# Projection units during the selection search made by seven products of quarters, with the sums on GpSimd

## The chip, the cores and the metric

The kernel runs on one core of one Trainium2 chip. The metric is the time of one execution on the device, in microseconds (us). The engines of a core are TensorE (PE, matrix products), VectorE (DVE), ScalarE (ACT), GpSimd (POOL) and SyncE (SP, which issues most of the transfers). PEld is TensorE's weight load. Each has its own queue of instructions and they meet by semaphores.

## The reference

One inference step of a one-layer decoder, all in float32: RWKV-7 time mixing beside sparse attention whose keys are selected by an indexer, merged by gates, and a gated feed-forward. What matters here is the projection of the 1104 rows (1040 of the prompt, 64 of the sample) and the selection of 256 keys for each prompt row.

```python
h = rms_norm(x, norm1_g) @ w_in              # 1104 x 1024 by 1024 x 5448
p_r, p_a, g_r, g_a = split_cols(h)           # 1792, 1608, 1024, 1024 columns
pm = p_r + (prev - p_r) * rwkv_mu            # prev is p_r one row earlier
sc = einsum('bqhd,bsd->bqhs', qi, ki) * D_IDX ** -0.5
score = einsum('bqhs,bqh->bqs', relu(sc), wi)
_, idx = lax.top_k(where(visible, score, -inf), 256)
out = attention over the selected keys only  # then time mixing, merge, feed-forward
```

## The kernel before

The change lies in one function, `prompt_and_project`, which in the profiled execution runs from about 224 us to 868 us. It does two things side by side: the indexer, the selection and the attention of the prompt rows; and, as work that TensorE can do in between, the part of the projection that gives p_r and both gates.

**The projection** is cut into 90 units. Unit u makes tile t = u // 3 (128 output columns, 30 tiles, of which the first NT = 14 are p_r and 16 are gates) for the column block j = u % 3 of the transposed input `xT` (3 blocks of 368 rows of the input, in `COLS`). A unit is 8 products of a 128x128 block of weights with a 128x368 block of `xT`, summed in one bank of PSUM (`unit`, L437). Weights come by pairs of tiles, 1 MB each, in two buffers `W` (`load`, L372; pair p waits until all units of pair p - 2 are multiplied). ScalarE takes a unit out of PSUM (`evacuate`, L592 for gates, L594 to L602 for p_r: once scaled by 1 - mu into `PMT`, once by mu, shifted by a row, into `PX`). GpSimd adds the two for a whole tile of p_r (L685, L686), and SyncE sends the tile to DRAM.

**The stage in order.** First the dots: 83 pieces of indexer products (L453 on TensorE, a Relu on ScalarE, L614, and a weighted sum on VectorE, L719 and L721), with units 0 to 3 put among them. Then the search: VectorE finds the 256th largest score of each row by 33 rounds over the bits of a float (`bisect`). A round counts the scores above a trial value: one count over the packed last block (L731), six over the other blocks (L736), then it reads the total of the packed one, which TensorE sums over the partitions with one product (`total`, L458, into `dp_PS`; VectorE's copy is L740), and three instructions on 7 values per partition set the next trial value (L755, L757, L760). TensorE meanwhile makes units 4 to 58, that is 55 units or 440 products ("steps"), and does `total(r)` after each 12 steps (`SPACING`), in an order written by hand; 44 steps remain after the last. Then VectorE turns the scores of the first three blocks into masks (`choose`, L773 to L781, L701), and the heads begin: scores, softmax, transposes and values for 65 heads in 33 teams, with the last 31 units between them (`fill_of`). `scores(0)`, the scores of the first head (L478), is put ahead of unit 4; the first head can go on when VectorE has done `peak_of(0)` (L814, L818), and `scores(1)` (L487) waits for that.

A product in float32 stands in the records as two MATMUL and two LDWEIGHTS entries, so 12 steps are x24 there.

The feed-forward of this kernel already makes some of its products in the way that the change brings here: seven products of quarters in place of eight (`block3`, L2313), with part of the sums on GpSimd.

## Time and profile before

| | |
|---|---|
| median of 3 runs | 2758.52 us (2755.36 to 2760.30) |
| the profiled execution, its own time | 2736.69 us |
| its span, first to last instruction | 2734.9 us |
| mean granted TensorE clock | 0.965 |
| busy: PE, DVE, ACT, POOL | 95%, 64%, 29%, 14% |
| all units (L437), busy | 465.9 us |
| the counts of the search (L736), busy | 176.0 us |

The profile is of one execution, 21.8 us below the median of the others (2758.52 - 2736.69). Its page lists busy time by engine, the granted clock by slice, the chain of work that ended last, and groups of instructions; below it are answers of its trace: stretches with the busy time of each engine, timelines, and groups by line and shape. An engine that is 95% busy over the span can still wait at given places, and it is these places that tell what an edit there is worth. "Idle before" in brackets names what the engine waited for.

### The profile page before, as it was taken

Reading aid. Unit: us, or ns where it says so; the run is one execution under the profiler, and the core shown is the slowest. Engines: PE = TensorE matmul, PEld = TensorE weight load, DVE = VectorE, ACT = ScalarE, POOL = GpSimd, SP = SyncE. Lnnn points to the kernel's source line nnn. Section 1 sums busy time; section 2 is a strip of 40 time slices with the busy share of each in tenths; the row PEclk is TensorE's granted clock in tenths of the full one; section 3 lists DMA queues with packets and bytes.
Section 4 is the critical chain, followed back from the end, with each engine's and each line's share of the span. In section 5 each row is a group of like instructions: output and inputs, shape, how many; then the busy total and the mean of one; then the engine's idle time right before and its main releaser. Section 6 shows DMA issues by size and latency. Waiting matters only on the chain.

```text
span 2734.9 us, 49325 instructions
## 1 busy us (share of the span) xinstructions
PE 2589.1 (95%) x19336; PEld 1788.2 (65%) x19336; DVE 1739.7 (64%) x3313; ACT 788.5 (29%) x1725; POOL 391.4 (14%) x574
## 2 busy tenths in 40 slices
PE   8998999999997997898889999998999999999997
PEld 5553566666654323788756997655656666579997
DVE  3555888874533448666668999988762322357666
ACT  2224322124443653111112553012335321221212
POOL 0000111000000000000001663000335441011111
PEclk9999999999998986999999999999999999999999
DMA  8882112131113450000144664443337563533332
GB/s 297 308 292 86 41 64 88 65 103 37 49 41 106 178 162 27 4 27 12 66 146 160 234 241 167 133 122 129 106 133 242 180 201 117 173 124 123 124 124 72
DMA packets 95961, 348.79 MB, mean 128 GB/s; under 512 B 19561, under 2 KB 43977, under 8 KB 74033
## 3 DMA queue, kind: packets, MB, share of 16 engines
q1 hardware_dynamic: 83696, 294.50, 31.3%
q0 software_dynamic: 12032, 51.14, 5.8%
q8 instruction: 153, 2.51, 0.4%
q14 instruction: 80, 0.65, 0.1%
HBM read 289.57 MB, written 55.23 MB: 126 GB/s over the span
## 4 chain that ended last, share of the span: by engine, by line
PE 47%; DVE 7%; DVEq 3%; issue 1%; DMA 1%; POOL 0%; ACT 0%; POOLq 0%; ACTq 0%; SPq 0%
PE banks L2368 6%; PE banks L2281 5%; PE tl_P L2368 4%; PE banks L2313 4%; PE banks L2299 3%; PE tl_P L2313 3%; PE rc_P L1395 3%; PE banks L2213 3%; PE tl_P L2281 2%; DVE arena L2907 2%; DVEq L2905 2%; PE tl_P L2299 2%; DVE tl_v L2901 1%; PE tl_P L2213 1%; PE banks L1407 1%
## 5 line engine op out<-in xcount | busy, mean ns | idle before, releaser
L437 PE MATMUL dp_PS<-base,dp_W 128*128 128x368 f32 x1440 | 465.9, 476 | 0.0
L437 PEld LDWEIGHTS dp_PS<-base,dp_W 128*128 128x128 f32 x1440 | 265.8, 190 | 157.5 <-issue 8.8
L162 PE MATMUL pa_PG<-pa_W,base 128*128 128x402 f32 (+1 forms) x576 | 198.5, 504 | 7.8 <-DMA pa_W<-in_w_dsa 7.7
L736 DVE TENSOR_SCALAR_CACHE_REDUCE dp_EQ<-dp_SCORE,dp_trial 128x1024 f32<-128x1024 f32 (+1 forms) x186 | 176.0, 946 | 19.9 <-issue 0.9
L162 PEld LDWEIGHTS pa_PG<-pa_W,base 128*128 128x128 f32 (+1 forms) x576 | 106.7, 187 | 94.6 <-issue 14.2
L2281 PE MATMUL banks<-base,tl_WU 128*128 128x368 f32 x496 | 157.9, 475 | 0.8 <-DVE base L2960 0.8
L2299 PE MATMUL banks<-base,tl_WD 128*128 128x368 f32 x484 | 154.3, 474 | 0.0
L2901 DVE MAX8 tl_v<-arena 128x8 f32<-128x4100 f32 x32 | 141.8, 4431 | 3.4 <-issue 1.6
L2904 DVE FIND_INDEX8 tl_i<-tl_v,arena 128x8 uint32<-128x4100 f32 x32 | 141.5, 4423 | 0.0
L2907 DVE MATCH_REPLACE8 arena<-tl_v,arena 128x4100 f32<-128x4100 f32 x32 | 141.3, 4414 | 0.0
L2851 POOL DMA_INDIRECT arena<-in_cache_kv,tl_PHT x128 | 122.6, 958 | 109.9 <-PE tl_P L2447 73.8
L2281 PEld LDWEIGHTS banks<-base,tl_WU 128*128 128x128 f32 x496 | 94.0, 191 | 59.5 <-issue 2.8
L2299 PEld LDWEIGHTS banks<-base,tl_WD 128*128 128x128 f32 x484 | 90.5, 190 | 57.1 <-issue 3.7
L2553 ACT ACTIVATE arena<-base 128x368 f32<-128x368 f32 x44 | 22.1, 509 | 270.6 <-DVEq L2944 150.8
L814 DVE CUSTOM_DVE_ANT_0 dp_P<-dp_PS,dp_SCORE 128x1024 f32<-128x1024 f32 (+7 forms) x64 | 48.5, 758 | 66.7 <-PE dp_PS L487 58.8
L2313 PE MATMUL banks<-arena 128*128 128x184 f32 x504 | 85.6, 319 | 1.4 <-DVE arena L3075 1.4
L2225 PE MATMUL banks<-base,arena 128*128 128x368 f32 x256 | 81.3, 473 | 1.5 <-issue 1.1
L2313 PEld LDWEIGHTS banks<-arena 128*128 128x128 f32 x504 | 80.0, 190 | 1.6 <-issue 1.6
L2213 PE MATMUL banks<-arena 128*128 128x368 f32 x240 | 78.5, 480 | 1.1 <-DMA arena<-in_wb 1.1
L2281 PE MATMUL tl_P<-base,tl_WU 128*128 128x368 f32 x240 | 76.8, 473 | 0.0
L2520 POOL TENSOR_TENSOR base<-tl_T 128x368 f32<-128x368 f32 x36 | 30.6, 850 | 302.4 <-ACTq L2603 301.5
L594 ACT ACTIVATE dp_PMT<-dp_PS,dp_rest 128x368 f32<-128x368 f32 x42 | 23.8, 568 | 164.2 <-PE dp_PS L437 164.2
(525 smaller groups left out, 5077.1 us busy)
## 6 DMA issues: line engine op xcount, KB each, us to landing
tl_WU<-in_wu SPq DMA_DIRECT2D x58, 1024.0 KB, 4.9
pa_WQ<-in_wu SPq DMA_DIRECT2D x22, 1024.0 KB, 8.3
wsum<-pa_WS SPq DMA_DIRECT2D x22, 1024.0 KB, 4.9
tl_WD<-in_wd SPq DMA_DIRECT2D x32, 704.0 KB, 4.4
arena<-wsum SPq DMA_DIRECT2D x21, 1024.0 KB, 7.3
dp_W<-in_w_rw SPq DMA_DIRECT2D x15, 1024.0 KB, 5.5
arena<-in_wb SPq DMA_DIRECT2D x24, 512.0 KB, 3.8
arena<-in_wo SPq DMA_DIRECT2D x24, 512.0 KB, 3.8
```

Source lines behind the costliest of these rows:

```text
L162: last = pe.matmul(PG[0:n, c, 0:NC4], xT[:, k, r:r + n], W[:, c, k, :], start=k == 0, stop=k == KD - 1)
L437: last = pe.matmul(bank(f)[:, 0:w], W[:, t // 2 % 2, k, 128 * (t % 2):128 * (t % 2) + 128], xT[:, k, c:c + w], start=k == 0, stop=k == KD - 1)
L736: dve.tensor_scalar(EQ[0:n, 0:m], scored_of(j), values(n, x), None, op, ALU.add, accum_out=result[0:n, x:x + 1])
L2213: last = pe.matmul(out[:, 0:W], WM[:, i % 2, o:o + 128], YT[:, j, k, :], start=k == 0, stop=k == 3)
L2281: last = pe.matmul(out[:, 0:W], WU[:, i % 2, o:o + 128], XN[:, k, :], start=k == 0, stop=k == KD - 1)
L2299: last = pe.matmul(out[:, 0:W], WD[:, i % 3, 128 * e:128 * e + 128], HT[:, f, :], start=f == 0, stop=f == NF - 1)
L2313: last = pe.matmul(out[:, 0:H], weights[:, k, :], moving(k), start=first and k == 0, stop=k == 3, skip_group_check=True)
L2368: last = pe.matmul(out[:, 0:H], weights[:, k, :], moving(k), start=first and k == 0, stop=k == kk - 1, skip_group_check=True)
L2851: pool.indirect_dma_start(out=KV[:, n % 16, t, :], out_offset=None, in_=I["cache_kv"], in_offset=bass.IndirectOffsetOnAxis(ap=PHT[:, 64 * ...
L2901: dve.max(v8[:, :], SC)
L2904: dve.max_index(i8[:, :], v8[:, :], SC)
L2907: dve.match_replace(SC, v8[:, :], SC, TAKEN)
```

## The change

Units 4, 5 and 54 to 58 stay as they are. The 48 units from 6 to 53 (pairs 1 to 8, `PAIRS`) are made in 24 blocks. A block takes two tiles at once (units 6q + j and 6q + 3 + j) and makes them from quarters: weights of 512x128 and `xT` of 512x184. Seven products of four 128x128 by 128x184 multiplications each (28 in all) stand in for 16 of 128x368. Three of the seven accumulate onto another one in PSUM (`FA`, `FB`, `FD`; the fourth bank is `FE`; these are banks 0 to 3), so ScalarE copies a bank between two products (`keep`), and the second product goes on adding.

The sums that the seven products need are all made by GpSimd:

- `mix_rows(j)`, once per column block: four sums of 128x736 over `xT`, into `XF`. Blocks 0 and 1 at the very start of the stage, block 2 early in the search.
- `weights_a`, `weights_b`, `weights_c`, once per pair of tiles: four sums of 128x512, into `WF`.
- per block: `f16` and `f167` (two sums of 128x184) and `finish` (three sums of 128x184), after which ScalarE may run `evacuate` for the two units, now from `STG` in SBUF.
- `mix_tile(t)`, as before (L685 and L686), two for each pair while the pair after it is made.

The ticks that space the totals count 2 for each product of four multiplications, 1 for each step of a plain unit: 24 blocks x 14 + 56 = 392 in place of 440. `scores(0)` moves behind the last total. The buffers share memory: `RL`, `CUM`, `ones`, `P`, `PTS` and `YB` now lie in one array, `room_for`, over which `WF`, `f1` to `f167`, `STG` and `XF` lie too. So `ones` is filled after the search, and VectorE first waits there for the copies of units up to 53. The number of units among the heads stays 31.

```diff
+        PAIRS = range(1, AHEAD // 6)
+        BLOCKS = [(q, j) for q in PAIRS for j in range(3)]
+        by_seven = lambda u: u // 6 in PAIRS
...
+                def seven(m, tick):
...
+                    def multiply(out, weights, e, moving, first, made):
+                        for k in range(4):
+                            last = pe.matmul(out, weights(e, k), moving(k), start=first and k == 0, stop=k == 3,
+                                             skip_group_check=True)
+                        last.then_inc(made, 1)
+                        tick(2)
...
+                    pe.wait_ge(fa_taken, 2 * m - 2)
+                    multiply(FA, raw, 0, left, True, fa_made)
+                    pe.wait_ge(xf_made, j + 1)
+                    pe.wait_ge(wf_made, 3 * q - 2)
+                    pe.wait_ge(fb_taken, 2 * m - 2)
+                    multiply(FB, mixed_w, 1, mix(1), True, fb_made)
...
+                    multiply(FD, mixed_w, 0, mix(0), True, fd_made)
+                    pe.wait_ge(fa_taken, 2 * m - 1)
+                    multiply(FA, raw, 1, low_left, False, fa_made)
...
+                    multiply(FB, mixed_w, 2, mix(2), False, fb_made)
...
+                    multiply(FE, raw, 3, mix(3), True, fe_made)
+                    pe.wait_ge(wf_made, 3 * q)
+                    pe.wait_ge(fd_taken, 2 * m - 1)
+                    multiply(FD, mixed_w, 3, low_right, False, fd_made)
...
-                scores(0)
-                pe.wait_ge(same_in, 16)
-                steps = [(f, k) for f in range(AMONG, AHEAD) for k in range(KD)]
-                for i, (f, k) in enumerate(steps):
-                    unit(f, k, k + 1)
-                    if i % SPACING == SPACING - 1 and i // SPACING < ROUNDS:
-                        total(i // SPACING)
...
+                def tick(n):
+                    spent[0] += n
+                    if spent[0] >= SPACING * (spent[1] + 1) and spent[1] < ROUNDS:
+                        total(spent[1])
+                        spent[1] += 1
...
+                for m in range(1, NBL + 1):
+                    seven(m, tick)
+                for f in range(6 * PAIRS.stop, AHEAD):
+                    for k in range(KD):
+                        unit(f, k, k + 1)
+                        tick(1)
...
                 scores(0)
...
+                def keep_block(m):
+                    if m > 1:
+                        act.wait_ge(f_mid, m - 1)
...
+                    keep(f1, FA, fa_made, fa_taken, 2 * m - 1)
+                    keep(f6, FB, fb_made, fb_taken, 2 * m - 1)
+                    if m > 1:
+                        both(m - 1)
+                    keep(STG[:, 1, H:2 * H], FD, fd_made, fd_taken, 2 * m - 1)
+                    keep(STG[:, 0, 0:H], FA, fa_made, fa_taken, 2 * m)
+                    keep(f7, FB, fb_made, fb_taken, 2 * m)
...
+                def mix_rows(j):
+                    c = COLS[j][0]
+                    high, low, to = xT[:, 0:4, c:c + 2 * H], xT[:, 4:8, c:c + 2 * H], XF[:, j]
+                    pool.tensor_tensor(to[:, 0], high[:, :, H:], high[:, :, 0:H], ALU.subtract)
+                    pool.tensor_tensor(to[:, 2], low[:, :, H:], high[:, :, H:], ALU.subtract)
+                    pool.drain()
+                    pool.tensor_tensor(to[:, 1], low[:, :, H:], to[:, 0], ALU.subtract)
+                    pool.drain()
+                    pool.tensor_tensor(to[:, 3], low[:, :, 0:H], to[:, 1], ALU.subtract)
...
+                def finish(m):
+                    pool.wait_ge(fd_taken, 2 * m)
+                    pool.wait_ge(fe_taken, m)
+                    pool.tensor_tensor(STG[:, 0, H:2 * H], STG[:, 0, H:2 * H], f16, ALU.add)
+                    pool.tensor_tensor(STG[:, 1, H:2 * H], STG[:, 1, H:2 * H], f167, ALU.add)
+                    pool.tensor_tensor(STG[:, 1, 0:H], STG[:, 1, 0:H], f167, ALU.add)
+                    pool.drain().then_inc(f_done, 1)
...
+                mix_rows(0)
+                mix_rows(1)
                 pool.wait_ge(weighted, dots0[0] + len(pieces(0)) + 1)
...
+                mix_tile(0)
+                pool.wait_ge(weighted, len(all_pieces))
+                weights_a(PAIRS[0])
+                weights_b(PAIRS[0])
+                weights_c(PAIRS[0])
+                mix_tile(1)
+                mix_rows(2)
...
-                dve.memset(ones[:, :], 1.0)
                 pad()
...
                 bisect()
+                dve.wait_ge(copied, 6 * PAIRS.stop)
+                dve.memset(ones[:, :], 1.0)
+                dve.drain()
```

On TensorE, where the search begins: `dp_QZ` is the operand of `scores(0)`, `dp_part` and `dp_same` those of a total, `dp_W` a unit's weights. Before:

```order
L453 MATMUL dp_PS<-KIT,base 128x384 x3
L478 MATMUL dp_PS<-base,dp_QZ 128x512 x4
L478 MATMUL dp_PS<-base,dp_QZ 128x16 x2
L437 MATMUL dp_PS<-base,dp_W 128x368 x12
L458 MATMUL dp_PS<-dp_part,dp_same 128x1
```

and now (`dp_room_for` holds the sums of rows and weights):

```order
L517 MATMUL dp_PS<-KIT,base 128x384 x3
L463 MATMUL dp_PS<-base,dp_W 128x368 x12
L522 MATMUL dp_PS<-dp_part,dp_same 128x1
L463 MATMUL dp_PS<-base,dp_W 128x368 x4
L480 MATMUL dp_PS<-base,dp_W 128x184 x4
L480 MATMUL dp_PS<-dp_room_for 128x184 x8
L480 MATMUL dp_PS<-base,dp_W 128x184 x4
L522 MATMUL dp_PS<-dp_part,dp_same 128x1
```

The first total now stands 12 steps behind the last dot, with no scores between, and from the second on six products of four stand between two totals.

On TensorE, where the search ends. Before:

```order
L437 MATMUL dp_PS<-base,dp_W 128x368 x12
L458 MATMUL dp_PS<-dp_part,dp_same 128x1
L437 MATMUL dp_PS<-base,dp_W 128x368 x44
L487 MATMUL dp_PS<-base,QT 128x512 x4
L500 MATMUL dp_PS<-ident,dp_P 128x128 x8
```

and now:

```order
L463 MATMUL dp_PS<-base,dp_W 128x368 x12
L522 MATMUL dp_PS<-dp_part,dp_same 128x1
L463 MATMUL dp_PS<-base,dp_W 128x368 x8
L522 MATMUL dp_PS<-dp_part,dp_same 128x1
L542 MATMUL dp_PS<-base,dp_QZ 128x512 x4
L542 MATMUL dp_PS<-base,dp_QZ 128x16 x2
L551 MATMUL dp_PS<-base,QT 128x512 x4
L564 MATMUL dp_PS<-ident,dp_room_for 128x128 x8
```

The 44 steps between the last total and the second head's scores are gone; the six products of the first head's scores stand there instead.

On GpSimd, from the start of the stage. Before, with `dp_PMT` and `dp_PX` the two scaled copies of a tile:

```order
L675 MEMSET dp_PX 128x1 x2
L679 DMA dp_PACK<-dp_SCORE 16x130 x8
L685 TENSOR_TENSOR dp_PMT<-dp_PMT,dp_PX 128x1040
L686 TENSOR_TENSOR dp_PMT<-dp_PMT,dp_PX 128x64
```

and now, the first rows, and those of the first block of pair 2, with the two tiles of pair 1:

```order
L789 MEMSET dp_PX 128x1 x2
L795 TENSOR_TENSOR dp_room_for<-base 128x736
L796 TENSOR_TENSOR dp_room_for<-base 128x736
L798 TENSOR_TENSOR dp_room_for<-base,dp_room_for 128x736
L800 TENSOR_TENSOR dp_room_for<-base,dp_room_for 128x736
...
L817 TENSOR_TENSOR dp_room_for<-dp_W,dp_room_for 128x512
L857 TENSOR_TENSOR dp_room_for<-dp_room_for 128x184
L833 TENSOR_TENSOR dp_PMT<-dp_PMT,dp_PX 128x1040
L834 TENSOR_TENSOR dp_PMT<-dp_PMT,dp_PX 128x64
L864 TENSOR_TENSOR dp_room_for<-dp_room_for 128x184
```

The two rows of a tile's sum, which stood alone, now stand between the sums of the quarters, and two groups of four long sums stand ahead of everything.

## Rows read from the trace of the kernel before

**Rows 1.** Busy by stretch: us, each engine (instructions), clock, DMA, GB/s.

```profile
400.00:450.00 50.00, 50.00 (x171) 31.29 (x170) 43.28 (x119) 11.63 (x32) 7.27 (x6) 1.00 0.23 84
```

**Rows 2.** Timeline, one round: start, us, engine, line, operation, [idle before].

```profile
543.90 0.16 DVE L740 COPY dp_count<-dp_PS 128x1 f32<-128x1 f32 x1
544.13 0.17 DVE L755 TENSOR_SCALAR dp_step<-dp_count 128x7 int32<-128x7 f32 x1
...
545.33 0.38 PE L458 MATMUL dp_PS<-dp_part,dp_same 128*128 128x1 f32 x2
...
545.57 7.67 PE L437 MATMUL dp_PS<-base,dp_W 128*128 128x368 f32 x24
...
551.66 0.16 DVE L740 COPY dp_count<-dp_PS 128x1 f32<-128x1 f32 x1
```

**Rows 3.** Timeline, last dots and first search round, VectorE and TensorE.

```profile
303.91 4.05 PE L478 MATMUL dp_PS<-base,dp_QZ 128*128 128x512 f32 x12 [1.04 <-ACT dp_RL L614]
...
305.86 0.92 DVE L844 COPY base<-base 64x128 f32<-64x128 f32 x4
...
307.36 0.29 DVE L731 TENSOR_SCALAR_CACHE_REDUCE dp_EQ<-dp_PACK 128x130 f32<-128x130 f32 x1
...
315.63 0.16 DVE L740 COPY dp_count<-dp_PS 128x1 f32<-128x1 f32 x1 [1.99 <-PE dp_PS L458]
```

**Rows 4.** Timeline, end of the search and start of the heads.

```profile
560.97 27.45 PE L437 MATMUL dp_PS<-base,dp_W 128*128 128x368 f32 x88
...
588.38 1.24 DVE L814 CUSTOM_DVE_ANT_0 dp_P<-dp_PS,dp_P 128x1040 f32<-128x1040 f32 x1 [0.20 <-issue]
...
590.04 1.99 PE L487 MATMUL dp_PS<-base,QT 64*128 64x512 f32 x8 [1.61 <-DVEq L819]
```

**Rows 5.** Timeline of TensorE where seven products are already in use.

```profile
1508.11 1.41 PE L2313 MATMUL tl_P<-base,tl_WU 128*128 128x184 f32 x8
...
1516.83 1.41 PE L2313 MATMUL tl_P<-base,tl_WU 128*128 128x184 f32 x8
```

**Rows 6.** Timeline: a VectorE instruction beside one of GpSimd.

```profile
503.06 2.03 POOL L685 TENSOR_TENSOR dp_PMT<-dp_PMT,dp_PX 128x1040 f32<-128x1040 f32 x1 [12.62 <-ACTq L603]
503.13 1.98 DVE L755 TENSOR_SCALAR dp_step<-dp_count 128x7 int32<-128x7 f32 x1
```

**Rows 7.** Two small VectorE groups, 1495:1675: busy us, mean ns, idle.

```profile
L2908 DVE COPY arena<-tl_v 128x8 f32<-128x8 f32 x13 | 3.7, 284 | 0.0
L2909 DVE CAST arena<-tl_i 128x8 f32<-128x8 uint32 x13 | 3.3, 251 | 0.0
```

**Rows 8.** The first over the whole span, ns min/median/max; GpSimd, 1500:1600.

```profile
L2908 DVE COPY arena<-tl_v x32: 159/162/767, 1429.0 to 1950.3; 128x8 f32<-128x8 f32 x32
...
1500.00:1600.00 100.00, 62.49 (x93) 1.00 0.65 241
```

**Rows 9.** The counts of the search, ns min/median/max.

```profile
L736 DVE TENSOR_SCALAR_CACHE_REDUCE dp_EQ<-dp_SCORE,dp_trial x186: 611/946/1280, 316.9 to 558.7; 128x1024 f32<-128x1024 f32 x31, 128x896 f32<-128x896 f32 x31, 128x768 f32<-128x768 f32 x31, 128x640 f32<-128x640 f32 x31
```

**Rows 10.** Timeline: products weighted on VectorE beside a GpSimd sum.

```profile
286.50 2.46 POOL L685 TENSOR_TENSOR dp_PMT<-dp_PMT,dp_PX 128x1040 f32<-128x1040 f32 x1 [27.34 <-ACTq L603]
...
286.86 5.07 DVE L721 SCALAR_TENSOR_TENSOR dp_SCORE<-dp_RL,WI,dp_SCORE 128x128 f32<-128x128 f32 x7
```

**Rows 11.** Timeline, VectorE as the stage begins.

```profile
230.01 0.93 DVE L831 MEMSET dp_ones<- 128x1040 f32 x1 [7.32 <-DMA dp_later<-in_later]
```

**Rows 12.** Groups of GpSimd by shape: busy us, mean ns, idle before.

```profile
L685 POOL TENSOR_TENSOR dp_PMT<-dp_PMT,dp_PX 128x1040 f32<-128x1040 f32 x14 | 31.0, 2217 | 211.3 <-ACTq L603 211.3
...
L2800 POOL TENSOR_TENSOR arena<-arena 128x184 f32<-128x184 f32 x21 | 12.1, 577 | 4.4 <-ACT arena L2619 3.8 <-issue 0.5
...
L2030 POOL TENSOR_TENSOR arena<-tl_WU 128x512 f32<-128x512 f32 x1 | 1.3, 1265 | 117.2 <-DMA tl_WU<-in_wu 117.2
```

**Rows 13.** TensorE after a long idle: us, busy, clock, DMA, GB/s.

```profile
868.00:876.00 8.00, 0.33 (x4) 0.53 0.82 280
...
882.00:885.50 3.50, 3.50 (x16) 0.50 0.82 253
```

More of the change, by code:

```diff
@@ L603, in evacuate, with keep, both @@
                     act.drain().then_inc(copied, 1)
+                def keep(part, bank, made, taken, count):
+                    act.wait_ge(made, count)
+                    act.activation(part, bank, ACT.Copy).then_inc(taken, 1)
+                def both(m):
+                    q, j = BLOCKS[m - 1]
+                    act.drain()
+                    evacuate(6 * q + j)
+                    evacuate(6 * q + 3 + j)
+                def keep_block(m):
+                    if m > 1:
+                        act.wait_ge(f_mid, m - 1)
+                    else:
+                        act.wait_ge(weighted, len(all_pieces))
+                    keep(f1, FA, fa_made, fa_taken, 2 * m - 1)
[5 more added lines that the diff above has]
+                    keep(f7, FB, fb_made, fb_taken, 2 * m)
+                    keep(STG[:, 1, 0:H], FE, fe_made, fe_taken, m)
+                    keep(STG[:, 0, H:2 * H], FD, fd_made, fd_taken, 2 * m)
                 def rectify(j, p):
@@ L654, in _ @@
                         evacuate(d // EVERY)
-                for f in range(AMONG, AHEAD):
+                for f in range(AMONG, 6):
+                    evacuate(f)
+                for m in range(1, NBL + 1):
+                    keep_block(m)
+                both(NBL)
+                for f in range(6 * PAIRS.stop, AHEAD):
                     evacuate(f)
@@ new lines, in mix_tile @@
+                def mix_tile(t):
+                    px, pm = PX[:, t % 2], PMT[:, t % 2]
+                    seqs = px[:, 1 + TP:].rearrange("p (b q) -> p b q", q=9)
+                    later_rows = pm[:, TP:R].rearrange("p (b q) -> p b q", q=8)
+                    pool.wait_ge(copied, nth_copy(3 * t + 2) + 1)
+                    pool.tensor_tensor(pm[:, 0:TP], pm[:, 0:TP], px[:, 0:TP], ALU.add)
+                    pool.tensor_tensor(later_rows, later_rows, seqs[:, :, 0:8], ALU.add)
+                    pool.drain().then_inc(mixed, 1)
@@ L679, in _ @@
                     pool.dma_start(PACK[16 * x:16 * x + 16, :], SCORE[0:16, PW16 * x:PW16 * x + PW16]).then_inc(packed, 16)
[L680 to L687 removed]
+                mix_tile(0)
[5 more added lines that the diff above has]
+                mix_rows(2)
+                for m in range(1, NBL + 1):
+                    q, j = BLOCKS[m - 1]
+                    if m > 1:
+                        finish(m - 1)
+                        if j == 0:
+                            weights_c(q)
+                    pool.wait_ge(fa_taken, 2 * m - 1)
+                    pool.wait_ge(fb_taken, 2 * m - 1)
+                    pool.tensor_tensor(f16, f1, f6, ALU.add)
+                    if j == 0 and m > 1 and 2 * q - 2 < NT:
+                        mix_tile(2 * q - 2)
+                    if j == 2 and q + 1 in PAIRS:
+                        pool.wait_ge(fd_made, 2 * m - 1)
+                        weights_a(q + 1)
+                    pool.wait_ge(fb_taken, 2 * m)
+                    pool.tensor_tensor(f167, f1, f7, ALU.add)
+                    pool.drain().then_inc(f_mid, 1)
+                    if j == 0 and m > 1 and 2 * q - 1 < NT:
+                        mix_tile(2 * q - 1)
+                    if j == 2 and q + 1 in PAIRS:
+                        weights_b(q + 1)
+                finish(NBL)
                 pool.wait_ge(masked, 1)
@@ L692, in _ @@
                 gather_keys(pool, I, E, KX, kx_in, 0)
-                pool.wait_ge(product, NU)
+                pool.wait_ge(product, NU - 2 * NBL)
                 gather_keys(pool, I, E, KX, kx_in, 1)
```

101 lines of the change are left out of this document (78 added, 23 removed).

## The prediction

> **What bounds the kernel now.** I read the stretches first. In the search (about 307 to 567 us) TensorE is busy for the whole of its time and VectorE for 43.3 of 50 us [rows 1]. That looks like a TensorE bound, so I read one round in the timeline. VectorE reads the total at 543.90 and again at 551.66 without an idle time ahead of it: 7.76 us a round. TensorE's 12 steps between two totals are 7.67 us of records [rows 2]. What TensorE needs when nothing holds it shows in the first round: its steps begin behind a row that ends at 303.91 + 4.05 = 307.96, and VectorE, which waits for it there, has the total at 315.63, 7.67 us later [rows 3]. The difference to 7.76 is small, but VectorE has the longer round. So the chain of the search is VectorE's, and TensorE's steps are cover.
>
> Then the end. After the last total TensorE has 27.45 us of steps left, from 560.97 to 588.42, while VectorE counts, makes three masks and comes to the first head at 588.38. The next products of TensorE start at 590.04 after an idle time of 1.61 us put down to VectorE [rows 4]. So the heads begin when VectorE is ready; a shorter row of steps in front of them starts nothing earlier.
>
> **What is removed from TensorE.** Of 440 ticks 392 stay. Seven products run here already: one block of 28 lasts 1516.83 - 1508.11 = 8.72 us [rows 5], that is 14 ticks of 0.623 us. A plain step is (27.45 - 7.67) / 32 = 0.618 us, from rows of 44 and of 12 steps [rows 2, 4]. So a tick costs the same as before and a round still has 12 of them. The removed 48 ticks (30 us) all fall behind the last total, where VectorE sets the time [rows 4]. Worth: 0. TensorE will wait there for about 560.97 to 588, less the 4.05 us of the first head's scores, instead.
>
> **What moving the first scores gives.** They stand ahead of the first steps and cost 4.05 us; VectorE starts its first count at 307.36 and then waits 1.99 us for the total [rows 3]. With the steps 4 us earlier that wait goes. VectorE is next, so I count -2.0 us and not 4.
>
> **What GpSimd adds.** Each edit there costs nothing by itself; the question is who waits for it and whom it stops. For the second there are rows. At 503.13 a VectorE instruction on 7 values took 1.98 us in place of 0.17; a GpSimd sum ran from 503.06 to 505.09, and VectorE's ended 0.02 us behind it [rows 6]. In the dots, seven weighted sums of 128x128 took 5.07 us beside such a sum [rows 10]. Later, where GpSimd is busy for 62 of 100 us, two small VectorE instructions take 284 and 251 ns on average against a median of 162, in the worst case 767 [rows 7, 8]. The counts, which fill most of a round, show no such thing: the longest of 186 takes 1280 ns [rows 9]. So some VectorE instructions wait for a running GpSimd sum to its end: the three small ones of a round, the sums of two arrays, the small copies.
>
> The Trainium skill, page "SBUF — State Buffer", section "Who interferes with whom", says that copies, tensor_scalar without its accumulator and instructions with two SBUF inputs share a port pair with GpSimd, that whoever starts first keeps it for the whole instruction, and that the other blocks fully. It speaks against this change, and rows 6 agree. Taken at its word for each instruction it gives the upper price of the rounds below, 29 us, where rows 7 give 9 to 13.
>
> Now the places, with the durations of [rows 12]: a sum of 128x184 0.577 us, of 128x512 1.27, of 128x1040 2.22; so one of 128x736, which no row has, about 1.65 (between the last two, by length).
>
> 1. Start. `mix_rows(0)` and `mix_rows(1)` are eight sums of 1.65 us, 13 us and some gaps from about 224 on, to about 237. VectorE waits for a transfer until 230.01 [rows 11], so the first half is free. In the other 7 us it has seven small copies and sums to make and then the weighted sums, and gets about one in for each sum of GpSimd. The dots that follow are a chain of VectorE. Between 0 (GpSimd loses each time) and 7 (VectorE stands still); I take 5, nearer to the upper end, because seven short ones beside a single sum of 2.46 us are stretched to 5.07 [rows 10], and here the sums follow one another.
> 2. Start of the search. `weights_a` to `weights_c` are four sums of 1.27 us as soon as the last dot is weighted, when VectorE has seven short instructions to do, such as four copies in 0.92 us [rows 3]. Between 0 and 5; I take 3.5. Then `mix_rows(2)`, four sums of 1.65 us, meets the three small ones of one round: 0 to 5, I take 3.
> 3. The rounds. Blocks last 24 x 14 / 12 = 28 rounds. In three blocks (42 ticks, 3.5 rounds of 7.76 = 27.2 us) GpSimd has fifteen sums of 0.577, four of 1.27 and, for six pairs of eight, two of 2.22. An instruction that comes at any moment waits on average the sum of the squares of these over twice the time: (5.0 + 6.5 + 9.9) / 54.4 = 0.39 us with the long ones, 0.21 without. Three in a round, six pairs of eight: 3 x (0.75 x 0.39 + 0.25 x 0.21) = 1.04 us, times 28 = 29 us. The same sum for the stretch of [rows 7, 8], with some 5 sums of 0.577 and three of 0.9 in each 8.73 us, gives 0.24 us where the rows show (122 + 89) / 2 = 105 ns. By that ratio, 0.44, the rounds cost 13 us; by the 105 ns as they stand, 3 x 0.105 x 28 = 9 us. I take 15: near the rows, and a little over them, as the three come 0.24 us apart and can each meet the next sum of a row of sums. Range 9 to 29.
> 4. `ones`: 0.93 us less at the start [rows 11], 0.93 and a drain more behind the search. +0.1. Its wait for the copies of unit 53 costs nothing: block 24 ends at tick 352, in round 30 of 33.
>
> **The clock.** TensorE's wait of some 23 us (27.4 - 4.05) ahead of the heads is new. After such a gap in this trace the granted clock was 0.50 (1.2 GHz) while TensorE was nearly idle, and stayed there for 3.5 us of full work behind it [rows 13]. That costs half of 3.5 us, or up to 4 if it lasts twice that. Part lies beside the softmax of the first head. +2, range 0 to 4.
>
> **ScalarE** is busy 11.6 of 50 us in the search [rows 1]. Seven copies of 128x184 in a block, even at GpSimd's 0.577 us each [rows 12], bring it to some 6 of 9 us; hidden, unless it waits (rival C).
>
> **The sum.** -2.0 + 5 + 3.5 + 3 + 15 + 0.1 + 2 = +26.6 us. The profiled execution, 2736.7 us, would be 2763.3. The median of the runs before is 2758.52, 21.8 us above that execution; the difference belongs to no place that the trace shows, so I add the sum to the median: 2785.1 us. Ends: -2 + 0 + 0 + 0 + 9 + 0.1 + 0 = +7.1, that is 2765.6, and -2 + 7 + 5 + 5 + 29 + 0.1 + 4 = +48.1, that is 2806.6.
>
> **The rivals.**
> A. The waits behind GpSimd cost next to nothing, because its sums fall beside the counts, as they do now: of fourteen long sums [rows 12] two show someone waiting [rows 6, 10]. For it: the medians of [rows 8] are the undisturbed ones. Against: GpSimd's share goes from 7 of 50 us [rows 1] to two thirds. Then -2 to +5: 2757 to 2764, the same.
> B. It gets faster: TensorE is the bound of the search after all, by its full busy time [rows 1], and 48 ticks of 0.62 us come off. Then 2758.5 - 30 = 2728.5. It decides if the last total came late by TensorE; rows 2 and 4 speak against it, for VectorE waits for nothing there, and the ticks come off behind the last total.
> C. TensorE starves. In a block, the copy of product 3 must be made before product 7, and ScalarE gets to it only behind `both`, which waits for `finish` on GpSimd. If GpSimd and VectorE hold each other up so that a block comes 1 us later than the 9.05 us that VectorE's rounds leave it, 24 blocks add 24 us to the sum: 2809. For it: the long sums of `mix_tile` stand ahead of `finish` in that queue. Against: GpSimd's own work is 18 of 27 us by the prices above, and the same scheme ran at 8.72 us a block in [rows 5].
>
> **How the numbers follow.** Forecast (slower by 7 to 48 us) 0.73, C 0.12, A 0.10, B 0.05. A measurement of this kernel can tell 0.2% (5.5 us) from no change. Faster comes from B, same from A, slower from the forecast and C. The range leaves out B, most of A, and the far end of C: 2762 to 2812.
>
> **What the profile after would show.** The 33 counting rounds longer than 7.76 us on average, about 8.3, with L755, L757 and L760 (or the lines that they have then) at maxima of 0.5 to 2 us and each such end on the end of a GpSimd sum; the counts unchanged. The first weighted sum later than 232.96 by some 5 us. TensorE idle for some 20 us ahead of the heads, with a lower clock behind it. Blocks of 8.7 us with waits only at totals. If VectorE waits for totals in many rounds, C is right; if the small ones keep 0.17 us, A; if the heads start before 588 us by more than 3, B. I am wrong most easily in the 15 us of the rounds, since the phase between blocks and rounds is not random: rounds stand at seven fixed places of three blocks.

## The result, and the profile after

| | before | after |
|---|---|---|
| median | 2759.04 us (2755.36 to 2760.30) | 2777.45 us (2774.77 to 2779.04) |
| ratio | 1 | 1.0074, 95% interval 1.0059 to 1.009 |
| the profiled execution, its own time | 2736.69 us | 2778.36 us |
| its span | 2734.9 us | 2776.6 us |

The change made the kernel slower by 18.4 us (16.3 to 24.8 by the interval), where 26.6 were forecast. The two profiled executions lie 41.7 us apart. The second half of that comes from a place far behind the change, and the last part of this section takes it out.

**Where it comes from.** I put the same instruction side by side in both traces (us from the start of the span; starts).

| anchor | before | after | later by |
|---|---|---|---|
| first weighted sum | 232.96 | 235.61 | 2.6 |
| last weighted sum | 304.6 | 308.4 | 3.8 |
| first count (L731, after L914) | 307.36 | 315.20 | 7.8 |
| first total read (L740, after L923) | 315.63 | 321.56 | 5.9 |
| last total read, 32 rounds on | 567.3 | 585.3 | 18.0 |
| first mask | 567.8 | 587.0 | 19.2 |
| first head on VectorE (L814, after L997) | 588.38 | 607.62 | 19.2 |
| second head's scores (L487, after L551) | 590.04 | 609.27 | 19.2 |
| last product of the stage | 868.1 | 888.5 | 20.5 |

Stage start, the timeline of after (start, us, engine, line, operation, idle before). Before, the four copies took 0.54 us, the two 0.39 and the first weighted sum 0.49:

```profile
229.78 2.08 DVE L976 COPY dp_QZ<-QT 64x32 f32<-64x32 f32 x4
229.80 1.75 POOL L800 TENSOR_TENSOR dp_room_for<-base,dp_room_for 128x736 f32<-128x736 f32 x1
...
232.18 3.02 DVE L983 COPY dp_QIZ<-base 64x64 f32<-64x64 f32 x2
...
235.61 1.76 DVE L902 TENSOR_SCALAR dp_SCORE<-dp_room_for,WI 128x512 f32<-128x512 f32 x1
```

VectorE's small instructions are held one at a time: one of the four copies took 1.71 us and ended 0.03 us behind the sum at 229.80, and the two 64x64 copies (1.33 and 1.68 us) ended 0.05 us behind the sums after it. Start of the search, VectorE and GpSimd, after; it answers to [rows 3], where L844, now L1026, took 0.92 us:

```profile
311.76 1.89 DVE L1026 COPY base<-base 64x128 f32<-64x128 f32 x4
313.66 1.17 DVE L1028 COPY base<-KIT 128x64 f32<-128x64 f32 x1
...
321.56 0.16 DVE L923 COPY dp_count<-dp_PS 128x1 f32<-128x1 f32 x1
```
```profile
312.00 1.34 POOL L813 TENSOR_TENSOR dp_room_for<-dp_W 128x512 f32<-128x512 f32 x1 [0.18 <-issue]
313.51 1.27 POOL L817 TENSOR_TENSOR dp_room_for<-dp_W,dp_room_for 128x512 f32<-128x512 f32 x1 [0.18 <-issue]
```

The first total is read without an idle time ahead of it; the 1.99 us of [rows 3] are gone. Two rounds of the search, after:

```profile
428.59 0.16 DVE L923 COPY dp_count<-dp_PS 128x1 f32<-128x1 f32 x1
428.83 1.05 DVE L938 TENSOR_SCALAR dp_step<-dp_count 128x7 int32<-128x7 f32 x1
...
430.20 1.09 DVE L943 TENSOR_SCALAR dp_trial<-dp_bits 128x7 int32<-128x7 int32 x1
...
438.52 0.16 DVE L923 COPY dp_count<-dp_PS 128x1 f32<-128x1 f32 x1 [0.43 <-issue]
438.76 0.44 DVE L938 TENSOR_SCALAR dp_step<-dp_count 128x7 int32<-128x7 f32 x1
...
439.51 2.23 DVE L943 TENSOR_SCALAR dp_trial<-dp_bits 128x7 int32<-128x7 int32 x1
```
```profile
428.58 1.27 POOL L807 TENSOR_TENSOR dp_room_for<-dp_W 128x512 f32<-128x512 f32 x1 [0.25 <-PE dp_PS L480]
430.00 1.27 POOL L809 TENSOR_TENSOR dp_room_for<-dp_room_for,dp_W 128x512 f32<-128x512 f32 x1
...
438.59 0.58 POOL L857 TENSOR_TENSOR dp_room_for<-dp_room_for 128x184 f32<-128x184 f32 x1 [0.24 <-issue]
439.33 2.38 POOL L833 TENSOR_TENSOR dp_PMT<-dp_PMT,dp_PX 128x1040 f32<-128x1040 f32 x1 [0.17 <-ACTq L687]
```

L938 ends at 429.88 and L807 at 429.85; L943 at 431.29 and L809 at 431.27; L943 at 441.74 and L833 at 441.71. Over the whole search the three small lines and the counts, ns min/median/max:

```profile
L938 DVE TENSOR_SCALAR dp_step<-dp_count x31: 170/172/1051, 329.4 to 578.0; 128x7 int32<-128x7 f32 x31
```
```profile
L943 DVE TENSOR_SCALAR dp_trial<-dp_bits x30: 170/172/2226, 330.1 to 570.7; 128x7 int32<-128x7 int32 x30
```
```profile
L919 DVE TENSOR_SCALAR_CACHE_REDUCE dp_EQ<-dp_SCORE,dp_trial x186: 612/946/1280, 322.9 to 577.1; 128x1024 f32<-128x1024 f32 x31, 128x896 f32<-128x896 f32 x31, 128x768 f32<-128x768 f32 x31, 128x640 f32<-128x640 f32 x31
```

The medians are as before, the maxima are not, and the counts are those of [rows 9]. All 33 small instructions of 0.2 us or more in the search end 0.02 to 0.03 us behind the end of a GpSimd instruction. I also added up, for the stretch from the first to the last read of a total, what the small instructions (128x7) took over 0.172 us each, VectorE's idle time put down to TensorE, and the idle time of its own issue:

| kernel | search, us | small ones over 0.172 us (how many took 0.2 us or more) | wait for TensorE | issue | rest |
|---|---|---|---|---|---|
| before | 251.66 | 1.83 (1 of 94) | 0.20 | 2.26 | 247.37 |
| after | 263.71 | 14.29 (33 of 94) | 0.00 | 1.72 | 247.70 |

So a third of the small instructions carry the 12.05 us (263.71 less 251.66); the rest is only 0.33 us apart. GpSimd is busy for 32.3 of 50 us here, against 7.3 in [rows 1]:

```profile
400.00:450.00 50.00, 45.18 (x276) 43.93 (x275) 43.51 (x104) 21.23 (x65) 32.31 (x39) 0.97 0.23 80
```

The end of the search, after, in the timeline, and the stretches behind the second head's scores (us, PE, PEld, DVE, ACT, POOL, clock, DMA share, GB/s):

```profile
586.00 0.93 DVE L1032 MEMSET dp_room_for<- 128x1040 f32 x1 [0.32 <-issue]
...
607.62 1.24 DVE L997 CUSTOM_DVE_ANT_0 dp_room_for<-dp_PS,dp_room_for 128x1040 f32<-128x1040 f32 x1 [0.20 <-issue]
...
609.27 3.78 PE L551 MATMUL dp_PS<-base,QT 64*128 64x512 f32 x8 [24.37 <-DVEq L1002]
```
```profile
609.00:613.00 4.00, 3.73 (x9) 1.29 (x9) 1.02 (x3) 1.25 (x2) 0.00 (x0) 0.50 0.02 4
613.00:617.00 4.00, 3.73 (x19) 2.57 (x18) 2.77 (x6) 1.46 (x3) 0.00 (x0) 0.97 0.00 0
```

TensorE's idle time in front of L551 is 24.37 us where it was 1.61 [rows 4]: most of the 30 us taken off TensorE is here, as a hole. Behind it the clock is 0.50 (1.2 GHz) for 4 us; the same scores took 1.99 us in [rows 4] and take 3.78 now.

**The other 21 us.** From L2313's last product to L2281's last, far behind the stage, the trace of before has 471.5 us and that of after 492.8. A 50 us window there, of after, then of before:

```profile
2071.00:2121.00 50.00, 30.52 (x115) 18.75 (x116) 6.07 (x20) 12.59 (x26) 22.03 (x24) 0.76 0.55 173
```
```profile
2050.00:2100.00 50.00, 46.77 (x245) 29.60 (x245) 13.04 (x45) 23.44 (x49) 30.68 (x32) 0.97 0.77 245
```

In the window of after TensorE is idle for 19.5 us. The rows put 13.9 us of that down to its own issue, such as this one; one wait for a transfer (3.2 us) and one for ScalarE (2.9 us) stand there too:

```profile
2090.37 0.47 PE L2466 MATMUL banks<-base,tl_WU 128*128 128x368 f32 x1 [2.24 <-issue]
```

All nine experiments below have the long form too (493.5 to 494.5 us), the two made from the kernel before among them. So it is not the change; the profiled execution of before, 22 us faster than the median, was one without it. Like for like the change costs 20.5 us by the traces (the last anchor, which lies ahead of that place) and 18.4 by the medians.

### The profile page after: what moved, and what is told of

Its sections match the earlier page's. It is cut to its first block, busy times and chain, and to the rows that moved or that the text cites. A ratio compares the mean times of both kernels' runs of the same rounds, so it can differ in the third digit from the quotient of the medians.

```text
span 2776.6 us, 51076 instructions
## 1 busy us (share of the span) xinstructions
PE 2575.7 (93%) x19912; PEld 1855.8 (67%) x19912; DVE 1762.9 (63%) x3313; ACT 843.2 (30%) x1893; POOL 520.1 (19%) x738
## 4 chain that ended last, share of the span: by engine, by line
PE 48%; DVE 6%; DVEq 2%; issue 1%; another core or an unknown queue 1%; DMA 1%; ACT 0%; POOL 0%; ACTq 0%; POOLq 0%; SPq 0%
PE banks L2553 6%; PE banks L2466 5%; PE tl_P L2553 4%; PE banks L2498 4%; PE banks L2484 3%; PE tl_P L2498 3%; PE rc_P L1580 2%; PE banks L2398 2%; PE tl_P L2466 2%; PE banks L2410 2%; DVE arena L3092 2%; DVEq L3090 2%; PE tl_P L2484 2%; DVE tl_v L3086 1%; PE banks L1592 1%
## 5 line engine op out<-in xcount | busy, mean ns | idle before, releaser
L463 PE MATMUL dp_PS<-base,dp_W 128*128 128x368 f32 x672 | 222.2, 477 | 1.0 <-ACT dp_room_for L723 1.0
L919 DVE TENSOR_SCALAR_CACHE_REDUCE dp_EQ<-dp_SCORE,dp_trial 128x1024 f32<-128x1024 f32 (+1 forms) x186 | 176.0, 946 | 19.5 <-issue 0.5
L463 PEld LDWEIGHTS dp_PS<-base,dp_W 128*128 128x128 f32 x672 | 122.1, 190 | 74.3 <-issue 8.8
L480 PE MATMUL dp_PS<-dp_room_for 128*128 128x184 f32 x576 | 100.5, 324 | 0.0
L480 PEld LDWEIGHTS dp_PS<-dp_room_for 128*128 128x128 f32 x576 | 92.1, 192 | 0.0
L997 DVE CUSTOM_DVE_ANT_0 dp_room_for<-dp_PS,dp_SCORE 128x1024 f32<-128x1024 f32 (+7 forms) x64 | 48.5, 758 | 68.2 <-PE dp_PS L551 60.8
L691 ACT ACTIVATE dp_room_for<-dp_PS 128x184 f32<-128x184 f32 x168 | 51.0, 325 | 113.0 <-PE dp_PS L480 107.1
```

What stands on the lines that cost most here:

```text
L463: last = pe.matmul(bank(f)[:, 0:w], W[:, t // 2 % 2, k, 128 * (t % 2):128 * (t % 2) + 128], xT[:, k, c:c + w], start=k == 0, stop=k == KD - 1)
L480: last = pe.matmul(out, weights(e, k), moving(k), start=first and k == 0, stop=k == 3, skip_group_check=True)
L919: dve.tensor_scalar(EQ[0:n, 0:m], scored_of(j), values(n, x), None, op, ALU.add, accum_out=result[0:n, x:x + 1])
```

## The experiments

Ratios are to runs of the kernel before made beside each kernel on the same chip, with medians of 2755.1 us (e1, e2, e3, e7), 2755.4 (e4, e5, e8) and 2753.6 (e11, e12); for the change itself it was 2759.04. So compare kernels by their ratios, not by their medians. The search is the stretch between the first and the last read of a total, and the other columns are from one trace each.

| kernel | median, us | ratio, 95% interval | first total read | search | second head's scores | last product of the stage |
|---|---|---|---|---|---|---|
| after | 2777.45 | 1.0074 (1.0059 to 1.009) | 321.6 | 263.7 | 609.3 | 888.5 |
| e1_no_sums | 2758.0 | 1.0014 (1.0001 to 1.0027) | 312.7 | 256.8 | 593.5 | 873.4 |
| e2_psum_bits | 2761.26 | 1.0026 (1.0014 to 1.0038) | 322.0 | 250.8 | 596.8 | 875.6 |
| e3_later_sums | 2772.92 | 1.007 (1.0052 to 1.0088) | 313.5 | 268.5 | 606.0 | 885.1 |
| e4_six_ahead | 2760.22 | 1.0018 (1.0003 to 1.0033) | 321.9 | 264.9 | 610.8 | 872.9 |
| e7_before_short | 2759.82 | 1.0013 (1.0003 to 1.0023) | 315.5 | 251.4 | 589.7 | 868.9 |
| e8_psum_later | 2762.87 | 1.0033 (1.0017 to 1.0049) | 313.0 | 259.7 | 596.6 | 876.8 |
| e5_all | 2750.6 | 0.9983 (0.9971 to 0.9995) | 313.1 | 260.5 | 601.2 | 863.3 |
| e11_bits_six | 2746.0 | 0.997 (0.996 to 0.998) | 321.5 | 250.3 | 597.6 | 856.8 |
| e12_before_six | 2765.56 | 1.0043 (1.0031 to 1.0055) | 315.0 | 251.4 | 617.8 | 877.3 |

**e1_no_sums: are GpSimd's sums the cause?**

```diff
 def mix_rows(j):
-    pool.tensor_tensor(to[:, 0], high[:, :, H:], high[:, :, 0:H], ALU.subtract)
...
+    if j == 0:
+        pool.memset(XF[:, 0].rearrange("p i k n -> p (i k n)"), 0.0)
...
-    pool.tensor_tensor(f16, f1, f6, ALU.add)
...
-    pool.tensor_tensor(f167, f1, f7, ALU.add)
```

> The changed kernel with every sum that GpSimd makes for the seven products left out (mix_rows, weights_a to weights_c, f16, f167, finish; one fill of XF stands in for the first). All waits, products and copies stay, so the units are wrong. Theory (VectorE waits behind GpSimd's sums): rounds of the search back at 7.76 us, the first head (608 us after, 588 us before) at about 587 us, the whole within 0.1% of before. Rival (the chain of products and copies is late, or the cover of TensorE is missed): rounds stay over 8 us and the first head beyond 600 us.

The second head's scores come 15.8 us earlier than in after, the ratio falls from 1.0074 to 1.0014. So the sums are most of it. The first head stands at 591.8, not at the 587 expected. What is left is 3.54 us of small instructions behind the long sums of `mix_tile` (the kernel before had 1.83), and a wait that was covered in after, 4.65 us on VectorE: it reads the total with TensorE late. TensorE, in the timeline of this kernel:

```profile
356.64 0.28 PE L522 MATMUL dp_PS<-dp_part,dp_same 128*128 128x1 f32 x2
358.08 1.49 PE L480 MATMUL dp_PS<-base,dp_room_for 128*128 128x184 f32 x8 [1.16 <-ACT dp_room_for L691]
```
```profile
356.22 0.31 ACT L670 ACTIVATE dp_PX<-dp_sh,dp_mu 128x8 f32<-128x8 f32 x1 [2.60 <-DMA PM_dram<-dp_PMT]
...
357.61 0.98 ACT L691 ACTIVATE dp_room_for<-dp_PS 128x184 f32<-128x184 f32 x4
```

Product 7 stands still because ScalarE copies product 3 only behind `evacuate`. That is rival C's place, but not its reason: GpSimd makes no `finish` sums here. ScalarE had waited 2.60 us for the transfer of an earlier tile to DRAM, whose buffer the new tile needs. The pair of rows comes five times, once in each of five pairs (TensorE waits 1.16 to 2.44 us, ScalarE for the transfer 2.60 to 3.99). This is read from the rows; no run took the transfer away.

**e7_before_short: would fewer steps behind the last total pay by themselves (rival B)?** In the kernel before, units 54 to 58 are one product in place of eight; the rest of these units is left out.

```diff
+if 54 <= f < AHEAD:
+    if end == KD:
+        pe.matmul(bank(f)[:, 0:w], W[:, t // 2 % 2, 0, 128 * (t % 2):128 * (t % 2) + 128],
+                  xT[:, 0, c:c + w], start=True, stop=True).then_inc(product, 1)
+    return
```

> The kernel before with units 54 to 58 cut to one product each in place of eight: 35 of the 44 steps behind the last total are left out, nothing else. Theory (VectorE sets the start of the heads): the first head stays at 588 us; the heads lose at most 1 to 2 us by a lower clock after TensorE's wait; time within 0.1%. Rival (TensorE is the bound there): the heads begin 21 us earlier and the whole is 0.8% faster.

TensorE stops at 567.0 in place of 588.4. The first head does not move:

```profile
588.00 1.24 DVE L819 CUSTOM_DVE_ANT_0 dp_P<-dp_PS,dp_P 128x1040 f32<-128x1040 f32 x1 [0.20 <-issue]
```
```profile
589.66 3.60 PE L492 MATMUL dp_PS<-base,QT 64*128 64x512 f32 x8 [22.68 <-DVEq L824]
```

The scores take 3.60 us in place of 1.99, at a granted clock of 0.51 over 4 us, and the heads last 279.3 us (589.66 to 868.95) in place of 278.0. Rival B is out, and the price of TensorE's wait with the low clock behind it is 1.3 us, apart from the rest of the change. That is one pair of executions; in the other kernels here with such a gap (after, e1_no_sums, e2_psum_bits, e3_later_sums, e8_psum_later) the heads last 278.9 to 280.2 us.

**e2_psum_bits: is it the access to SBUF that the small ones wait for?** The step and the next bit go to bank 7 of PSUM; the third instruction becomes an exclusive or of two arrays, one of them there, and one memset of 7 values is added to a round. The work of GpSimd stays as it is.

```diff
+step_p, next_p = (PS[:, 7, c:c + NS].bitcast(I32) for c in (0, 16))
+dve.memset(next_p, 1 << max(b - 1, 0))
-dve.tensor_scalar(step[:, :], count[:, :], float(TOPK), float(1 << b), ALU.is_ge, ALU.mult)
+dve.tensor_scalar(step_p, count[:, :], float(TOPK), float(1 << b), ALU.is_ge, ALU.mult)
-dve.tensor_tensor(bits[:, :], bits[:, :], step[:, :], ALU.bitwise_xor)
+dve.tensor_tensor(bits[:, :], bits[:, :], step_p, ALU.bitwise_xor)
-dve.tensor_scalar(trial[:, :], bits[:, :], 1 << (b - 1), None, ALU.bitwise_xor)
+dve.tensor_tensor(trial[:, :], bits[:, :], next_p, ALU.bitwise_xor)
```

> The changed kernel with the three small instructions of a round taken off the shared reads and writes: the step and the next bit lie in PSUM, so each has one operand in SBUF only (one tiny fill more in a round). GpSimd's work is the same. Theory: they no longer wait for GpSimd's sums, rounds of 7.8 to 7.9 us in place of 8.24 on average, the first head about 11 us earlier (597 us), the whole 0.4% faster than the changed kernel. Rival (the rounds are long for another reason, such as late totals): rounds stay at 8.2 us.

The search takes 250.78 us, less than before the change: 0.10 us over in 1 of 94 small instructions, where after has 14.29 in 33. Two of the lines, ns min/median/max:

```profile
L940 DVE TENSOR_SCALAR dp_PS<-dp_count x31: 168/168/169, 329.9 to 565.5; 128x7 int32<-128x7 f32 x31
```
```profile
L945 DVE TENSOR_TENSOR dp_trial<-dp_bits,dp_PS x30: 161/162/163, 330.4 to 557.9; 128x7 int32<-128x7 int32 x30
```

They now run inside a sum of GpSimd, in the timeline of this kernel:

```profile
439.72 0.57 POOL L864 TENSOR_TENSOR dp_room_for<-dp_room_for 128x184 f32<-128x184 f32 x1 [0.18 <-issue]
439.73 0.16 DVE L942 TENSOR_TENSOR dp_bits<-dp_bits,dp_PS 128x7 int32<-128x7 int32 x1
439.97 0.16 DVE L945 TENSOR_TENSOR dp_trial<-dp_bits,dp_PS 128x7 int32<-128x7 int32 x1
```

The wait belongs to instructions with all their arrays in SBUF. One array of it in PSUM frees them, and 12.9 us of the 20.5 are back. Of the rest, 6.4 us lie ahead of the first total (322.0 against 315.6).

**e3_later_sums: the dots and the first weights.** `mix_rows(1)` and the first `weights_a` to `weights_c` wait until VectorE has made its small copies.

```diff
 mix_rows(0)
-mix_rows(1)
...
-pool.wait_ge(weighted, len(all_pieces))
+pool.wait_ge(indexed, 1)
 weights_a(PAIRS[0])
 weights_b(PAIRS[0])
 weights_c(PAIRS[0])
+mix_rows(1)
 mix_tile(1)
 mix_rows(2)
```

> The changed kernel with mix_rows(1) taken out of the dots and the first weights_a to weights_c held until VectorE has done its small copies ahead of the search; both now run under the first rounds. Theory: the dots end 4 to 5 us earlier (as before the change), the search begins 4 us earlier, a part comes back as waits in the first rounds (1 to 3 us): the first head at about 601 us. Rival: the rows for block 2 come too late and TensorE, then VectorE, waits: no gain.

The first total is read 8.1 us earlier, at 313.5, and the last only 3.3 us earlier; the first head comes at 604.3, where 601 was expected. The long sums meet the first rounds instead: these last 9.49 and 10.15 us, with small instructions such as

```profile
314.50 1.63 DVE L934 TENSOR_SCALAR dp_trial<-dp_bits 128x7 int32<-128x7 int32 x1
```
```profile
324.40 1.62 DVE L940 TENSOR_TENSOR dp_bits<-dp_bits,dp_step 128x7 int32<-128x7 int32 x1
```

In all 17.55 us over in place of 14.29, and 2.22 us of waits for TensorE. The ratio, 1.007, cannot be told from that of the change. A collision that is moved is mostly paid elsewhere.

**e8_psum_later: both edits.**

> Both repairs without moving units: step and next bit in PSUM, and the first sums held until the search. Theory: dots as before the change (end at 304.5 us), search of 251 to 255 us (the small ones do not wait; TensorE's wait at product 7 for ScalarE may cost 1 to 3 us in the first rounds), the first head at about 588 to 590 us, as before the change; the whole 2757 to 2760 us. So the change without its collisions is worth nothing by itself. Rival: the whole is faster than before by more than 0.2%.

The two gains do not add up: the search lasts 259.7 us, not 251 to 255, and the time is that of e2_psum_bits alone (1.0033 against 1.0026, with intervals that overlap). The small ones are free (1.98 us over, in two instructions), but VectorE waits 7.74 us for TensorE, and TensorE waits for the chain ScalarE, GpSimd, in this kernel's timeline:

```profile
331.05 2.82 PE L480 MATMUL dp_PS<-base,dp_W 128*128 128x184 f32 x8 [4.71 <-ACT dp_room_for L691]
...
365.86 1.49 PE L480 MATMUL dp_PS<-base,dp_room_for 128*128 128x184 f32 x8 [1.83 <-ACT dp_room_for L691]
```
```profile
329.49 0.57 POOL L857 TENSOR_TENSOR dp_room_for<-dp_room_for 128x184 f32<-128x184 f32 x1 [0.24 <-issue]
330.02 0.57 POOL L864 TENSOR_TENSOR dp_room_for<-dp_room_for 128x184 f32<-128x184 f32 x1
```

The first block's `f16` and `f167` (L857, L864) stand behind thirteen long sums of GpSimd and end at 330.59. ScalarE may not overwrite `f1` until then, and the product at 331.05, the fourth of block 2, adds onto the bank that ScalarE has to copy into it. The later rows, at product 7, are those of e1_no_sums. Once VectorE is not the late one, both show.

**e4_six_ahead: is TensorE's freed time worth anything?** Six teams of heads go without a unit, and these six units are made ahead of the heads, 65 in all.

```diff
-return int(m >= 256 or x < NTEAM - 2)
+return int((m >= 256 or x < NTEAM - 2) and x not in (2, 7, 12, 17, 22, 27))
```

> The changed kernel with six units taken out of the heads (teams 2, 7, 12, 17, 22, 27 hold none) and made ahead: 65 units ahead in place of 59, three of the blocks more and one pair more by seven products, 434 ticks. TensorE's wait of 24 us ahead of the heads is filled. Theory (the 48 ticks saved are worth what the heads give up): the heads lose 6 x 5.1 us of products and end about 28 us earlier against their start, the first head comes 1 to 3 us later by three more blocks of GpSimd's sums: the whole about 27 us below the changed kernel, 2750 us, 0.3% below before. Rival (the heads are not bound by TensorE, the units among them fill waits): less than 10 us gained.

It gives 0.56% back (ratio 1.0018 in place of 1.0074, some 15.4 us), not the 28 expected. The heads last 262.1 us in place of 279.3. Their 48 products less are 29.7 us of TensorE at 0.618, and TensorE is busy 27 us less there; 10 us come back as idle time. The rows name the softmax, such as:

```profile
773.63 0.66 PE L564 MATMUL dp_PS<-ident,dp_room_for 128*128 128x128 f32 x4 [1.14 <-DVEq L1011]
777.85 1.09 PE L580 MATMUL dp_PS<-dp_room_for,V 128*64 128x128 f32 x16 [1.58 <-ACTq L746]
```

**e5_all: e8_psum_later with six units more ahead, as in e4_six_ahead.**

> Both repairs and six units fewer among the heads. Theory: the first head at 588 to 592 us, the heads 28 us shorter, the whole about 2731 us, 1.0% below before. Rival: TensorE, now without room in the search, delays the totals (a block waits at product 7), and half of it or more is lost.

The first of these kernels that is faster than before, by 0.17%, but 20 us behind its expectation. The search keeps the 8.57 us of waits for TensorE, the heads give 17 and not 28, and the first head comes 24.2 us behind the first mask in place of 20.6: its scores stand behind the 38 steps that are left after the last total (x76 in the row) and end at 599.54.

```profile
572.01 23.74 PE L463 MATMUL dp_PS<-base,dp_W 128*128 128x368 f32 x76
595.59 3.95 PE L542 MATMUL dp_PS<-base,dp_QZ 128*128 128x512 f32 x12
```

**e11_bits_six: each lesson applied.** GpSimd's sums stay where the change put them, the bits are in PSUM, six units more are ahead, and the first scores stand right behind the last total.

```diff
 for f in range(6 * PAIRS.stop, AHEAD):
     for k in range(KD):
         unit(f, k, k + 1)
         tick(1)
+        if spent[1] == ROUNDS and not asked:
+            pe.wait_ge(fa_taken, 2 * NBL)
...
+            scores(0)
+            asked = True
-for r in range(spent[1], ROUNDS):
-    total(r)
...
-scores(0)
```

> The change with two edits more: the next bit and the step of a round lie in PSUM, and six units more (65 in all) are made ahead of the heads, with the first head's scores right behind the last total and not behind the last unit. Theory (VectorE's small instructions wait for GpSimd in the rounds, and TensorE's freed time is worth something only if heads' units move into it): the search as with the bits in PSUM alone, 250 to 252 us, so the first head at 595 to 597, not held up by its scores; the heads 262 us in place of 279; so 17 us below the run with the bits in PSUM alone: about 2744, ratio to before 0.996. If the early scores hold up the totals or the units behind them, the second head's scores come behind 599 and the gain is 12 us or less: 2749. If the heads gain nothing because their softmax sets the time: 2761.

As expected within 2 us: 2746.0 us, 0.997 of before (0.996 to 0.998). The search takes 250.3 us with no wait for TensorE. TensorE's row behind the last total now reaches 1.7 us too far: the second head's scores start 3.4 us behind the first head (594.19), against 1.65 in the kernels where TensorE is free by then:

```profile
569.37 4.03 PE L542 MATMUL dp_PS<-base,dp_QZ 128*128 128x512 f32 x12
573.25 23.74 PE L463 MATMUL dp_PS<-base,dp_W 128*128 128x368 f32 x76
597.58 1.99 PE L551 MATMUL dp_PS<-base,QT 64*128 64x512 f32 x8 [0.59 <-ACTq L688]
```

The clock stays up too: the scores take 1.99 us. This version is faster than both kernels, by 0.3% against the kernel before.

**e12_before_six: was the seven-product form needed for that?** The kernel before with the same six units moved.

> The kernel before with six units more made ahead of the heads (65 in all), all by eight products. Theory (before, TensorE's row behind the last total, 27.45 us, just covers VectorE's masks; 48 steps more are bare): the second head's scores 28 to 30 us later, near 619, the heads 17 us shorter; slower than before by 11 to 13 us: about 2767, ratio 1.0044. Rival (the units among the heads are the cost and it was the seven products that made no difference): as fast as the change with this edit, 2755 or less.

Slower than before by 0.43%. The row behind the last total is now bare:

```profile
560.08 57.13 PE L437 MATMUL dp_PS<-base,dp_W 128*128 128x368 f32 x184
617.80 1.99 PE L487 MATMUL dp_PS<-base,QT 64*128 64x512 f32 x8 [0.59 <-ACTq L603]
```

The scores stand 27.8 us later, and 18.6 us come back in the heads. So the heads last the same in both kernels (259 us), and the change's 48 ticks are what makes room for the six units. This pair shows what the change is worth when VectorE does not pay for it: 2765.6 against 2746.0 us. The bits in PSUM, which e12_before_six lacks, can explain at most the 1.8 us that its search loses to held instructions. Against the kernel before as it was, the gain is 7.6 us.

## Why the prediction was right, and where its sizes were off

**The bound** (VectorE's chain, TensorE's steps as cover) held. For the row behind the last total e7_before_short and e12_before_six show it from both sides: 21 us less of TensorE gives nothing, 30 us more cost 28. In the search of after VectorE never waits for TensorE, and TensorE waits 8.4 us for VectorE's counts. "Worth: 0" for the 48 ticks was right, and so was the idle time in front of the heads ("some 23 us", 24.37 measured).

**The mechanism** (small VectorE instructions held for the length of a GpSimd sum, counts not) held, with the ends of the rows and with the PSUM version. The Trainium skill's page "SBUF — State Buffer", section "Who interferes with whom", names the port pair that the two engines share; these runs agree on who waits (tensor_scalar, tensor_tensor and copies of SBUF arrays, up to 2.23 us), and on counts with an accumulator not waiting (946 ns in the median, as before). Each term:

| term | forecast | measured |
|---|---|---|
| first total's wait gone | -2.0 | -1.9 (7.8 less 5.9) |
| (1) `mix_rows` in the dots | +5 | +4.7 (3.8, and the 0.93 of `ones` that left) |
| (2) first weights | +3.5 | +4.0 (7.8 less 3.8) |
| (2) `mix_rows(2)` and (3) the rounds | +18 | +12.1 (search), +12.5 in the small ones alone |
| (4) `ones`, at both ends | +0.1 | +0.3 (1.2 less 0.93) |
| the clock | +2 | +1.2 to 1.3 |
| sum | +26.6 | +20.5 in the trace, +18.4 in the medians |

The terms are read from one trace of each kernel, and VectorE's transfer at the start of the stage landed 0.6 us earlier in after, so single terms can be off by that much.

The terms that were too large are `mix_rows(2)` and the rounds. Two parts can be named. First, the kernel before already had 1.83 us of such collisions in the search, nearly all of it in [rows 6]; my sum priced the long sums of `mix_tile` again as if they were new. Second, `mix_rows(2)` was priced at 3 us for one round, and its last sum, up to 329.73, met instructions at 329.41 and 330.07 whose excess is 0.17 and 0.33 us, the second with sums of the block. What is left is 14.0 us for 28 rounds, 0.17 us for each small instruction (12.2 us and 0.15 us without what was there before). It lies between the 0.105 of [rows 7, 8] and the 0.35 that the formula's 29 us come to, and nearer to the rows, as chosen. The 15 us were a choice between two values, not worked out, so that they came within 1 us is in part luck. Whether the phase between blocks and rounds matters, which I named as the weak point, the trace leaves open: the rounds that begin at 353.96, 412.84 and 473.45, seven apart, last 7.99, 7.99 and 8.01 us, but those at 370.05, 428.59 and 489.22, seven apart too, last 8.85, 9.93 and 8.04.

**Rival C** had a right mechanism with no price here. Product 7 does wait for ScalarE, up to 1.79 us at a time in the trace of after (three times), but VectorE's longer rounds cover it: the wait for TensorE in its search is 0.00. It becomes real as soon as VectorE is quick: 4.65 us in e1_no_sums, 7.74 in e8_psum_later. Half of its reason was wrong: where `finish` was named, the rows at product 7 name the transfer of a tile. **Rival A** fell (33 of 94 instructions took 0.2 us or more), **rival B** too (e7_before_short).

**The median.** I wrote that the 21.8 us between the profiled execution and the median belonged to no place that the trace shows. One trace could not show it; beside the later ones it has a place, TensorE's idle time near 2090 us. Adding the sum to the median was right; comparing the two spans would have doubled the answer.

What stays open: what causes that idle place and makes it come and go between executions, and whether heads with fewer units could be ordered to lose less than the 10 us to the softmax.

## What to carry to other kernels

Work that is cut from one engine and put on GpSimd is not free for VectorE, even where GpSimd stood idle: look at which VectorE instructions are short, chained and entirely in SBUF, and put one operand of each into PSUM (12.9 us here). Time taken off an engine that is not late becomes a hole; move work into it (here six units from the heads: 0.56% or 15 us, both from after to e4_six_ahead and from e2_psum_bits to e11_bits_six), and keep what the next stage waits for ahead of the filler. After each such repair read again who is late: here it was VectorE, then TensorE behind ScalarE, its transfer and GpSimd's queue, then TensorE's own row behind the last total.

## What the runs showed of the hardware

- One operand in PSUM, input or output, was enough to let a 128x7 VectorE instruction run beside a GpSimd sum: at most 169 ns in 92 of them, against up to 2226 ns with all in SBUF.
- When both engines have rows of such instructions, VectorE gets a few small ones through between two sums, at times none, and the next is held to the end of the running sum: at the stage's start four copies of 64x32, 0.54 us before, took 2.08 us, and the two of 64x64 3.02 in place of 0.39. GpSimd's own 128x736 sums took 1.73 to 1.80 us.
- After 24 us without work TensorE's granted clock was 0.50 (1.2 GHz) for 4 us and 0.97 for the next 4; the stage was 1.2 to 1.3 us longer for it, less than the 1.8 us that the second head's scores alone lost. Probably the softmax beside it hid the rest; no run took it away.
- One place, near 2090 us, is 21 to 23 us longer in ten of the eleven profiled executions, mostly by idle time that the rows of TensorE put down to its own issue (13.9 of 19.5 us idle in the window of after). That is as much as the effect that was to be measured.
